# Background attention inside a gather loop: consumers on VectorE and ScalarE moved to stand two or three slots behind their producers

## The reference, cut to what matters

```
s_top, i_top = top_k(q . subkeys, 16)                 # two halves
c_top, c_idx = top_k(all sums of the halves, 16)
gate = softmax(c_top)
act  = gelu(u_tab[e] . x)                             # e: the chosen experts
y   += sum_k gate_k * act_k * v_tab[e_k]
a    = softmax(s0 + bias) - lam * softmax(s1 + bias)  # differential attention
```

## Time and profile before

| | |
|---|---|
| median of 3 runs | 3050.84 us (3049.5 to 3053.46) |
| profiled execution | 3048.28 us |
| its span | 3046.5 us |
| PE busy | 2329.2 us (76%) |
| DVE busy | 2079.3 us (68%) |
| ACT busy | 1363.4 us (45%) |
| POOL busy | 1186.2 us (39%) |
| DMA packets | 1156.82 MB, of which the gathers' queue 1078.73 MB |
| mean granted clock | 0.853 |

### The profile page before, as it was taken

One profiled execution on the slowest core, in us unless ns is written; L12 is line 12 of the kernel. 1 busy time (PEld: TensorE's weight loads), 2 busy tenths in 40 slices (PEclk: granted clock), 3 DMA queues, 4 the chain that ended last, 5 costly groups with the idle time before them and its releaser, 6 DMA issues.

```text
span 3046.5 us, 36181 instructions
## 1 busy us (share of the span) xinstructions
PE 2329.2 (76%) x11968; PEld 869.6 (29%) x11968; DVE 2079.3 (68%) x5054; ACT 1363.4 (45%) x4021; POOL 1186.2 (39%) x1078
## 2 busy tenths in 40 slices
PE   9877688877788788887778777777777777777665
PEld 6554322223233233332222222212222222222211
DVE  5763566687687787767867666666666666666664
ACT  2145344444545545544544444444444444444433
POOL 1010334444444343443444444443444444444442
PEclk9987898888899999998979788878878888877876
DMA  6010899999999999999999999999999999999997
GB/s 233 34 63 19 331 426 425 426 426 426 424 414 374 396 386 420 398 399 395 417 391 427 426 426 426 426 427 425 423 426 424 426 421 419 426 427 425 423 424 315
DMA packets 174604, 1156.82 MB, mean 380 GB/s; under 512 B 20481, under 2 KB 25153, under 8 KB 40913
## 3 DMA queue, kind: packets, MB, share of 16 engines
q0 software_dynamic: 149168, 1078.73, 85.1%
q1 hardware_dynamic: 25248, 75.79, 6.4%
HBM read 1139.03 MB, written 15.41 MB: 379 GB/s over the span
## 4 chain that ended last, share of the span: by engine, by line
DMA 37%; PE 28%; ACT 11%; DVE 9%; issue 4%; POOL 1%; DVEq 0%; POOLq 0%; ACTq 0%
DMA ring<-table,e_even 20%; DMA ring<-table,e_odd 17%; PE acc L1844 14%; PE qq_ps L1817 6%; DVE ring L1604 5%; PE acc L1939 2%; ACT diag L1331 2%; ACT weight L1324 2%; ACT L1424 2%; PE proj L1791 2%; ACT L1317 1%; ACT gelu L1424 1%; DVE wide L1619 1%; PE acc L1888 1%; ACT wide L1355 1%
## 5 line engine op out<-in xcount | busy, mean ns | idle before, releaser
L1844 PE MATMUL acc<-ring,diag 64*64 64x512 f32 x8192 | 1318.9, 727 | 638.5 <-ACT diag L1331 618.6
L1127 POOL DMA_INDIRECT ring<-table,e_even x512 | 591.1, 1155 | 785.1 <-PE acc L1844 714.5
L1127 POOL DMA_INDIRECT ring<-table,e_odd x512 | 569.4, 1112 | 760.8 <-PE acc L1844 720.9
L1604 DVE CUSTOM_DVE_ANT_0 ring<-ring,xn_even 128x1024 f32<-128x1024 f32 x512 | 626.5, 1224 | 324.2 <-DMA ring<-table,e_even 163.5
L1604 DVE CUSTOM_DVE_ANT_0 ring<-ring,xn_odd 128x1024 f32<-128x1024 f32 x512 | 626.0, 1223 | 311.4 <-DMA ring<-table,e_odd 153.7
L1424 ACT ACTIVATE gelu<-dots 128x1 f32<-128x1 f32 x1024 | 205.5, 201 | 1219.6 <-DVE dots L1604 1211.4
L1844 PEld LDWEIGHTS acc<-ring,diag 64*64 64x64 f32 x8192 | 245.7, 148 | 1426.2 <-ACT diag L1331 1235.7
L1331 ACT ACTIVATE diag<-pairs,weight 128x64 f32<-128x64 f32 x1024 | 356.1, 348 | 33.5
L1817 PE MATMUL qq_ps<-wq_rest,xnT_cur 128*128 128x256 f32 x736 | 220.1, 438 | 0.0
L1817 PEld LDWEIGHTS qq_ps<-wq_rest,xnT_cur 128*128 128x128 f32 x736 | 144.7, 212 | 148.4 <-issue 131.2
L1324 ACT ACTIVATE weight<-gelu,gate_even 128x1 f32<-128x1 f32 x512 | 150.7, 294 | 16.7
(11 more groups left out here) (267 smaller groups left out, 2242.9 us busy)
## 6 DMA issues: line engine op xcount, KB each, us to landing
wide<-w_units SPq DMA_DIRECT2D x26, 512.0 KB, 8.9
wq_rest<-wq SPq DMA_DIRECT2D x11, 1024.0 KB, 9.4
ring<-table,e_even POOLq DMA_INDIRECT x512
ring<-table,e_odd POOLq DMA_INDIRECT x512
w_own<-w_units SPq DMA_DIRECT2D x10, 512.0 KB, 6.8
h_next<-x SPq DMA_DIRECT2D x8, 512.0 KB, 17.7
wide<-w_out SPq DMA_DIRECT2D x2, 2048.0 KB, 8.9
wide<-w_out SPq DMA_DIRECT2D x1, 4096.0 KB, 16.3
```

The lines of the kernel that those rows point to most:

```text
L1127: pool.indirect_dma_start(out=ring[:, g % RING, :], out_offset=None, in_=table[:, :], in_offset=bass.IndirectOffsetOnAxis(ap=e_row[m % 2][ ...
L1604: dve.tensor_tensor_reduce(ring[:, g % RING, 0:D], ring[:, g % RING, 0:D], xn[(m // PH) % 2][:], 1.0, 0.0, ALU.mult, ALU.add, dots[:, k:k ...
L1844: ins = pe.matmul(acc[ACC_OF[t]][ROWS[j], HALF[i]], diag[ROWS[i], g % DIAGS, :], ring[ROWS[i], g % RING, D + j * 512:D + (j + 1) * 512], s ...
```

## The change

The semaphores and the operations stay as they are. Only the slots at which they stand in the four loops move. By offset o in the frame:

| engine | operation | before | after |
|---|---|---|---|
| DVE | biased, chunks 0, 1, 2 | 1, 3, 5 | 2, 4, 6 |
| DVE | maxima | 5 | 6 |
| ACT | exponentials | 6 | 7 |
| DVE | difference | 9 | 10 |
| PE | transposes, part 0 | 10 | 11 |
| ACT | weights_out, parts 0, 1 | 11, 13 | 13, 15 |
| PE | output part 0, transposes part 1 | 12 | 13 |
| PE | output part 1 | 14 | 15 |
| ACT | output_out | 15 | 1 of the next frame |
| DVE | head_sums | 1 | 3 |
| ACT | head_root | 6 | 4 |
| PE | transposed_head | 8 | 7 |
| DVE | head_output | 9 | 10 |

The channel groups move by `at`: centre 39 to 41, squares 40 to 41, variances 41 to 42, roots 42 to 45, inverse 43-46 to 47-50, divide 47 to 51, output 48 to 52.

```diff
@@ ScalarE
-                    if o == 6 and 0 < u <= UNITS and u % LATE == 0:
+                    if o == 4 and 0 < u <= UNITS and u % LATE == 0:
                         head_root(u // LATE - 1)
                     if k == 4 and m + 1 < NSTEPS:
                         gate_exp(m + 1)
                     if 0 <= u < UNITS:
-                        if o == 6:
+                        if o == 7:
                             exponentials(u)
-                        elif o in (11, 13):
-                            weights_out(u, (o - 11) // 2)
-                        elif o == 15:
-                            output_out(u)
+                        elif o in (13, 15):
+                            weights_out(u, (o - 13) // 2)
+                    if o == 1 and 0 < u <= UNITS:
+                        output_out(u - 1)
...
-                    if at == 40:
+                    if at == 41:
                         channel_squares(c)
-                    elif at == 42:
+                    elif at == 45:
                         channel_roots(c)
-                    elif at == 48:
+                    elif at == 52:
                         channel_output(c)
@@ VectorE
-                    elif at == 39:
+                    elif at == 41:
                         centre(c)
-                    elif 43 <= at < 47:
-                        inverse(c, at - 43)
-                    elif at == 47:
+                    elif 47 <= at < 51:
+                        inverse(c, at - 47)
+                    elif at == 51:
                         divide(c)
                     if 0 < u <= UNITS and u % LATE == 0:
-                        if o == 1:
+                        if o == 3:
                             head_sums(u // LATE - 1)
                         elif o == 7:
                             head_scale(u // LATE - 1)
-                        elif o == 9:
+                        elif o == 10:
                             head_output(u // LATE - 1)
                     if 0 <= u < UNITS:
-                        if o in (1, 3, 5) and o // 2 < len(chunks(TILES[u])):
-                            biased(u, o // 2)
-                        if o == 5:
+                        if o in (2, 4, 6) and o // 2 - 1 < len(chunks(TILES[u])):
+                            biased(u, o // 2 - 1)
+                        if o == 6:
                             maxima(u)
-                        elif o == 9:
+                        elif o == 10:
                             difference(u)
@@ PE
-                    if o == 8 and 0 < u <= UNITS and u % LATE == 0:
+                    if o == 7 and 0 < u <= UNITS and u % LATE == 0:
                         transposed_head(u // LATE - 1)
                     if 0 <= u < UNITS:
...
-                        elif o == 10:
+                        elif o == 11:
                             transposes(u, 0)
-                        elif o == 12:
+                        elif o == 13:
                             output(u, 0)
                             transposes(u, 1)
-                        elif o == 14:
+                        elif o == 15:
                             output(u, 1)
...
-                    elif at == 41:
+                    elif at == 42:
                         group_variances(c)
```

## The result

The changed kernel takes **3015.7 us** (median of 4 runs, 3014.9 to 3018.5) against 3050.4 for the kernel before: ratio 0.9886, 95% interval 0.9869 to 0.9903, so 34.7 us less. The profiled execution took 3015.5 us with a span of 3013.7.

What follows compares the result with a forecast made beforehand. DMA engines kept full by the gather stream were taken as the bound; of 17 us standing in the attention 5 were left, and 12 off the runs' median of 3050.8 gave 3039 us, range 3033 to 3053 (forecast proper 3033 to 3045).

Steps and rivals of the forecast that it cites:

- What bounds the kernel: Expert phase: a stream of 1024 gathers; keeping DMA engines full sets the end, savings count only where they stood still.
- about 17 us of standing DMA engines is all that a better order can win here: Background attention, 809 to 1540 us: DMA share below 1.01 summed to 16.5 us, give or take 4.
- the rest of the lower GB/s is small packets at a full share: Background attention: the remaining drop in DMA rate comes from small packets, which the change leaves as they are.
- I leave a third: Attention frames: 5 of the 17 us stay because a 4.5 us ScalarE block remains; 12 us are won.
- the waits of L1619: VectorE's waits for the scores in the attention: 95.1 us in 33 waits, mostly vanishing, about 10 us left.
- PE waiting for weights_out in the same slot: PE at output, now sharing a slot with the weights_out that feeds it: 0 to 0.5 us, 32 times.
- PE's waits for ScalarE's diagonals: PE in the attention: waits for the diagonal as long as 3 us and as many would show the prediction wrong.
- The worst lag grows by 0.7: ScalarE at offsets 6 and 7: its worst lag rises from 3.0 to 3.7 us and comes one slot later.
- mix_t's load: SyncE's queue after the attention: the load leaves 8 us later, PE waits 0 to 4 us once, cost 0.
- Rival (a): Attention frames: the ScalarE block was the whole cause, so 0 to 3 us are won, 3049; chance 0.21.
- Rival (b): Offsets 6 to 9: split table loads are passed on to the gathers, 41 us uncovered, giving 3075; chance 0.11.
- the clock would drop less often: PE in the attention: its clock dropping less often was a sign of the prediction being right.

Runs made afterwards that it cites:

- e_block_7: Changed kernel with two more one-column activations (Sqrt, Sigmoid) behind the exponentials at offset 7, lengthening that ScalarE block: 3039.3 us, ratio 0.9963.
- d: Changed kernel with gate_exp at k == 5 instead of 4, sharing one table load with the exponentials: 3014.7 us, ratio 0.9884.
- f: Changed kernel with one Sqrt of one column at offset 8, two more table loads a frame as a block of its own: 3016.4 us, ratio 0.9891.
- the front alone: Kernel before with biased, maxima, exponentials and difference one slot later, everything behind shifted one slot at its old distances: 3024.3 us, ratio 0.992.
- the back alone: Kernel before with only the unit's second half moved: weights_out at 13 and 15, output_out at 1, head_sums at 3: 3030.1 us, ratio 0.9942.
- with the head and the channel groups: Changed kernel with biased, maxima, exponentials, difference and the first transposes at the places of before: 3020.5 us, ratio 0.9897.

## Why the prediction was right or wrong, step by step

**What bounds the kernel: right**, and so was the direction. Only what kept DMA engines from their work was won, in the frames of the attention and nowhere else.

**The step that failed is "about 17 us of standing DMA engines is all that a better order can win here", with the sentence behind it, "the rest of the lower GB/s is small packets at a full share".** The standing part was right (17.5 measured, 14.7 of it won). The rest was not small packets: those cost some 5 us, before and after, and 28.1 us lay in stretched packets of 8 KB, of which 20.9 were won. The number was in the earlier trace rows all along: 398, 398, 402 and 400 GB/s against 425 are 12 + 11 + 10 + 11 = 44 us of missing bytes. By the kernel after, whose small packets are the same, 731 x (1 - 418 / 425) = 12 us is about what small packets and remaining dips make, so 32 us could be won. The Trainium skill (Perfetto Trace Analysis, DMA Engine Tracks) says that each DMA engine's slices show actual busy time, without idle. The packet times of this trace don't measure work alone, since the same 149168 packets took 22 us less; what fills the added time of a stretched packet, no run here shows.

**"I leave a third" was wrong too.** What is left of the standing is 2.8 us of 17.5, not 5 of 17, and 7.2 of 28.1 of the stretching. 44 less 12, all of it won, would have given 3019, but the 12 is read from the kernel after; by the earlier trace rows alone the loss was 44 us, and how much of it a better order could win was open.

**The parts.** VectorE: the waits of L1619 fell from 95.1 to 3.4, against 10 forecast; L1660's are gone. PE waiting for weights_out in the same slot, 0 to 0.5 us 32 times: it is 8.0 us in 9 waits, so the sum was bounded well, though a single one is up to 1.0. PE's waits for ScalarE's diagonals, named as a sign of being wrong if they stayed as long and as many, fell from 117 to 81 and from 142.1 to 122.8 us, but the longest is 5.1 and was 4.6. ScalarE: 19 more table loads before gelu (108 against 89 on the page), 16 before the exponentials and one more elsewhere, 36 in all where 34 were forecast; blocks of 4.6 and 3.0 where 4.5 and 2.9. "The worst lag grows by 0.7": counted from offset 6, landing-to-reissue rises by 5.9 us to its peak before and by 6.7 after, 0.8 more, as forecast; what the sum missed is that it starts from 7.8 and not from 11.4. No drain beside a load, idle 0.8 us before 47 of them. SP: counted from the last gather of the attention, mix_t's load leaves 6.2 us later (8 forecast) and PE begins 0.7 later; the stretch behind the attention is as long as before: cost 0 as said. That the clock would drop less often was wrong: by the trace's record of the granted clock it stood at half for 134 of the 783 us before and for 130 of the 751 after.

**Rival (a)**, the block as the whole cause, is out: the block stayed and the loss went. But its place was right, e_block_7 shows that 3 us more of it bring 23 us back. **Rival (b)**, the split tables, is out: d and f show 32 loads fewer or more to make no difference, as long as they don't lengthen one block. Its condition (landing to reissue above some 16 us at offset 8) didn't come about: in the changed kernel it is 12.6 there.

What the prediction lacked was the **coupling**: it added up waits as if each had its own price. Shown is that the parts don't add up: the front alone gives 25 us, the back alone 18 to 20 and with the head and the channel groups 30, all together 35. Shown too is that the gain goes with the peak of the lag. My reading, which the lag curves bear out but no run proves: a wait of VectorE or ScalarE for a late PE delays the dots or diagonals that PE needs next, which keeps PE late; break that in one half of the frame, and the lag drains before the next block.

## What to carry to other kernels

Judge a gather stream by its bytes a second against its best stretch, not by the busy share of the DMA engines: here, starved engines partly looked busy. In a software pipeline written out by hand across in-order engines, count the slots by which a consumer stands behind its producer, and give it more than the producer's real lag: one slot where two were needed gave nothing or nearly so. On an engine that feeds such a pipeline, extra time in short pieces was free here where one long block wasn't.

## What the runs showed of the hardware that I had not expected

A gather packet of 8 KB is recorded as 309 ns at the 5th to the 75th percentile in every stretch, and as up to 775 ns (99th percentile in the attention before, 342 after) when the queue runs dry. And PE's idling often cost twice: behind 3.92 us of it the combine took 1.98 us instead of the 1.09 of the row below, from the same frame, and in e_block_7 again behind 6.01 us. In the attention of the kernel before, PE idled for over 2 us 37 times, and 28 times the clock was granted at half (1.2 GHz) somewhere in the 6 us behind it; 9 times it wasn't.

```profile
1380.36 1.09 PE L1844 MATMUL acc<-ring,diag 64*64 64x512 f32 x8 [0.25 <-ACT diag L1331]
```
